# Grouped attention's projections as rounded products of 512 columns, with six heads of a row tile handled at once

## The reference

```
lat = split_cols((rms_norm_2(h, norm_g) * (1 + scale) + shift) @ w_in)      # 2048 rows
cx  = split_cols((rms_norm_2(hc, norm_g) * (1 + scale_c) + shift_c) @ w_in) # 256 context rows
# gqa_branch: 4 query heads (256 columns), 2 key heads (128), 2 value heads (128), 64 wide
ql = apply_rope(rms_norm_2(to_heads(q_l, 4), q_g), cos, sin)
kl = apply_rope(rms_norm_2(to_heads(k_l, 2), k_g), cos, sin)
vl = to_heads(v_l, 2)
kc = rms_norm_2(to_heads(k_c, 2), k_g); vc = to_heads(v_c, 2)
# apply_rope: x1, x2 = even, odd columns -> x1*cos - x2*sin, x1*sin + x2*cos
```

## Time and profile before

| | |
|---|---|
| time, median of 3 runs | 5102.38 us (5096.63 to 5104.45) |
| the profiled execution, its own time | 5105.85 us |
| span of its trace | 5104.0 us |
| PE (TensorE) busy | 4619.4 us, 91% |
| DVE busy | 2552.7 us, 50% |
| ACT busy | 1812.8 us, 36% |
| POOL busy | 1248.8 us, 24% |
| mean granted TensorE clock | 0.957 of full speed |

### The profile page before, as it was taken

How to read it: one execution, slowest core, us unless ns; L and a number is a source line. 1 busy time by engine, 2 the same in 40 slices (tenths; PEclk the granted TensorE clock), 3 DMA queues, 4 the chain that set the end, 5 groups by cost and what they waited for, 6 DMA issues and landing times. The chain is left out here.

```text
span 5104.0 us, 69099 instructions
## 1 busy us (share of the span) xinstructions
PE 4619.4 (91%) x26793; PEld 3262.8 (64%) x26793; DVE 2552.7 (50%) x5079; ACT 1812.8 (36%) x3472; POOL 1248.8 (24%) x1295
## 2 busy tenths in 40 slices
PE   6998998997969988999998998999898999989989
PEld 3447776775758656844556776877666745556767
DVE  3332245666644656445554474444655545533654
ACT  3332224663344111224444443243112224444431
POOL 1000022103410111418882000001222448850000
PEclk8999999998979999899999999999998999999999
DMA  5011103344420000100000202310000100002122
GB/s 198 8 41 71 61 1 129 135 154 163 154 95 26 1 10 1 59 15 11 11 11 29 74 29 87 91 38 17 1 10 20 48 9 11 11 14 71 44 83 91
DMA packets 150104, 272.24 MB, mean 53 GB/s; under 512 B 11756, under 2 KB 83092, under 8 KB 148116
## 3 DMA queue, kind: packets, MB, share of 16 engines
q1 hardware_dynamic: 145460, 257.34, 15.0%
q10 hardware_dynamic: 4320, 10.49, 0.6%
HBM read 198.50 MB, written 69.29 MB: 52 GB/s over the span
## 5 line engine op out<-in xcount | busy, mean ns | idle before, releaser
L1549 PE MATMUL ps_proj<-features_high,weights_high 128*128 128x512 f32 (+1 forms) x1168 | 470.9, 403 | 53.1 <-DVE features_low L1615 50.6
L1549 PE MATMUL ps_proj<-features_high,weight_ring_low 128*128 128x512 f32 (+1 forms) x1168 | 450.6, 386 | 0.0
L1549 PE MATMUL ps_proj<-features_low,weights_high 128*128 128x512 f32 (+1 forms) x1168 | 443.9, 380 | 0.0
L1615 DVE TENSOR_TENSOR features_low<-h_t,features_high 128x512 fp32r<-128x512 f32 (+2 forms) x300 | 224.3, 758 | 253.0 <-ACT features_high L1579 252.4
L1615 DVE TENSOR_TENSOR features_low<-features_or_outputs,features_high 128x512 fp32r<-128x512 f32 (+1 forms) x248 | 199.9, 816 | 228.0 <-ACT features_high L1579 227.5
L1549 PEld LDWEIGHTS ps_proj<-features_high,weights_high 128*128 128x128 f32 x1168 | 222.5, 190 | 120.9 <-issue 39.0
L1766 PE MATMUL ps_s<-qf,kb 64*128 64x128 f32 x3264 | 235.7, 285 | 60.8 <-DVE scores_t L1936 55.4
L1579 ACT ACTIVATE features_high<-h_t 128x512 fp32r<-128x512 f32 (+2 forms) x300 | 198.7, 665 | 257.8 <-PE ps_proj L1549 231.2
L2553 ACT ACTIVATE weight_ring<-ps_st 128x1024 f32<-128x1024 f32 x193 | 197.8, 1025 | 250.6 <-PE ps_st L2439 242.7
L1766 PEld LDWEIGHTS ps_s<-qf,kb 64*128 64x128 f32 x3264 | 200.8, 188 | 111.9 <-issue 59.2
L1579 ACT ACTIVATE features_high<-features_or_outputs 128x512 fp32r<-128x512 f32 (+1 forms) x248 | 176.3, 714 | 227.8 <-PE ps_proj L1549 202.4
(11 more groups left out here) (440 smaller groups left out, 10230.7 us busy)
## 6 DMA issues: line engine op xcount, KB each, us to landing
weight_ring<-in_w_in_dram SPq DMA_DIRECT2D x40, 1024.0 KB, 5.9
weight_ring<-in_w_mod_dram SPq DMA_DIRECT2D x48, 512.0 KB, 4.2
x_res<-h_rows SPq DMA_DIRECT2D x32, 512.0 KB, 4.2
res<-result SPq DMA_DIRECT2D x48, 264.0 KB, 2.1
res_rows<-res SPq DMA_DIRECT2D x48, 264.0 KB, 3.9
h_t<-v_rows SPq DMA_DIRECT2D x3, 4096.0 KB, 13.8
q_rows<-q_rows SPq DMA_DIRECT2D x34, 256.0 KB, 2.6
x_rows<-in_x_dram SPq DMA_DIRECT2D x16, 512.0 KB, 9.5
```

The costliest lines, as they stand in the source:

```text
L1549: mm = pe.matmul(bank[:, 0:n], w_[:, k0 + k, i * P:(i + 1) * P], f_[:, k, 0:n], start=start, stop=stop)
L1615: dve.tensor_tensor(self.fl[:, s % NB, :, 0:n], self.hT[:, k0:k0 + KS, c0:c0 + n], self.fh[:, s % NB, :, 0:n].bitcast(F32), ALU.subtract). ...
```

## The change

`stage_qkv2` now goes over 18 row tiles, each with all six heads and the values side by side in one PSUM bank of 512 columns. The products become split ones. A tile has two steps of four feature chunks; a step has for every chunk one product of 512 columns with `features_high`, two of 256 columns with the low weights (the ring holds the two groups apart), and one of 512 with `features_low`. `features_high` and `features_low` have two buffers, one step each, so the pair for a step can be made only when the step two before it is done. The high weights of both groups are made at the start of the stage. Queries are computed for all 18 tiles in both layers.

On ACT the new work is `rounded(s)` (high features of a step) and, once, four copies of weights; on DVE it is `low_step(s)` and, once, four subtractions:

```
+            rounded(0)
+            for half in range(2):
+                ks = slice(half * KS, (half + 1) * KS)
+                for g in range(2):
+                    w = env.group_here(act, g0 + g)
+                    act.activation(wh[:, ks, g * GC:(g + 1) * GC], w[:, ks, :], ACT.Copy).then_inc(whs.h, 1)
+            rounded(1)
...
+            def low_step(s):
+                t, k0 = s // 2, KS * (s % 2)
+                dve.wait_ge(fhs.h, fhs.at(s + 1))
+                if s >= 2:
+                    dve.wait_ge(stp.h, stp.at(s - 1))
+                dve.tensor_tensor(fl[s % 2][:, :, :], hT[:, k0:k0 + KS, t * P:(t + 1) * P], fh[:, s % 2, :, :].bitcast(F32),
+                                  ALU.subtract).then_inc(fls.h, 1)
```

POOL's addition of a tile now comes in two parts, keys first, both behind the tile's power:

```
+            def add(t):
+                pool.wait_ge(rp.h, rp.at(t + 1))
+                for g, dst, h0, nh in ((1, nat[:, t % NK, :], 4, 2), (0, qn[:, t % NQ, :], 0, 4)):
...
+                    pool.tensor_tensor(dst.rearrange("p (h x e) -> p h x e", x=2, e=HD), twice(ta), twice(tb), ALU.add).then_inc(st.h, 1)
+
+            for t in range(WT):
+                pool.wait_ge(mn.h, mn.at(t + 1))
+                pool.tensor_tensor(ss[:, 2, t, :], ss[:, 1, t, :], env.mhalf[:, :].to_broadcast([P, NH]), ALU.pow).then_inc(pw.h, 1)
+                if t >= 1:
+                    add(t - 1)
```

More of the change, by code:

```diff
@@ L2094, in stage_hgrn_norm, with stage_qkv2 @@
         s_.base += c_
-def stage_qkv2(env, layer, hT, q_d, room, spare, KA, KB, VN, qtiles):
+def stage_qkv2(env, layer, hT, q_d, room, spare, KA, KB, VN, aT, qtiles):
     nc, A = env.nc, env.A
     g0 = env.next_group
[L2105 to L2108, removed]
+    NQ, NK, KS = 3, 4, 4
+    NH, HW = 6, 6 * HD
+    NS = 2 * WT
+    fhs, fls, whs, wls, stp = (env.sem(n) for n in ("features_high", "features_low", "weights_high", "weights_low", "step_mm"))
+    nrm, rp, st = env.sem("qk_normed"), env.sem("rope_read"), env.sem("rope_sum")
     sq, mn, pw, vv = env.sem("qk_sq"), env.sem("qk_mean"), env.sem("qk_rstd"), env.sem("v_kept")
@@ L2144, in _, with turn @@
         def _(pe):
[L2145 to L2149, removed]
+            def turn(t):
+                pe.wait_ge(st.h, st.at(2 * t + 2))
                 if t >= NK:
@@ L2154, in turn @@
                 mm.then_inc(tq.h, 1)
[L2156 to L2172, removed]
@@ L2176, in _, with rounded @@
+            for t in range(WT - 2, WT):
+                turn(t)
         @block.scalar
         def _(act):
[L2178 to L2181, removed]
+            def rounded(s):
+                t, k0 = s // 2, KS * (s % 2)
+                if s >= 2:
+                    act.wait_ge(stp.h, stp.at(s - 1))
+                act.activation(fh[:, s % 2, :, :], hT[:, k0:k0 + KS, t * P:(t + 1) * P], ACT.Copy).then_inc(fhs.h, 1)
@@ L2194, in _ @@
                 act.activation(KB[HD:HD + 1, kv, :].rearrange("p (t c) -> p t c", c=P), one, ACT.Copy)
[L2195 to L2205, removed]
+            for t in range(WT):
+                if t + 1 < WT:
+                    rounded(2 * t + 2)
+                act.wait_ge(stp.h, stp.at(2 * t + 2))
+                if t >= 1:
+                    act.wait_ge(mn.h, mn.at(t))
+                act.activation(s2, ps[t % 4][:, 0:HW], ACT.Square).then_inc(sq.h, 1)
+                act.activation(VN[:, t, :], ps[t % 4][:, HW:CH], ACT.Copy).then_inc(vv.h, 1)
+                if t + 1 < WT:
+                    rounded(2 * t + 3)
+                if t >= 3:
+                    high(t - 3)
+            for t in range(WT - 3, WT):
+                high(t)
         @block.vector
@@ L2227, in low @@
                    .then_inc(kl.h, 1)
[L2229 to L2244, removed]
+            low_step(0)
@@ new lines, in _ @@
+            for half in range(2):
+                ks = slice(half * KS, (half + 1) * KS)
+                for g in range(2):
+                    dve.wait_ge(whs.h, whs.at(2 * half + g + 1))
+                    raw, lo = (r[:, (g0 + g) % 2, ks, :] for r in (env.wring, env.wlow))
+                    dve.tensor_tensor(lo, raw, wh[:, ks, g * GC:(g + 1) * GC].bitcast(F32), ALU.subtract).then_inc(wls.h, 1)
+            low_step(1)
+            dve.wait_ge(ld.h, ld.at(16 * (1 + NH)))
+            v3 = lambda a: a.rearrange("p (h e) -> p h e", e=HD)
@@ new lines, in _ @@
+            v4 = lambda a: a.rearrange("p (h j x) -> p h j x", j=32, x=2)
+            for t in range(WT):
+                if t + 1 < WT:
+                    low_step(2 * t + 2)
+                dve.wait_ge(sq.h, sq.at(t + 1))
+                link(dve.tensor_reduce(ss[:, 0, t, :], v3(s2), AXX, ALU.add))
+                dve.tensor_scalar(ss[:, 1, t, :], ss[:, 0, t, :], 1.0 / HD, EPS, ALU.mult, ALU.add).then_inc(mn.h, 1)
+                if t + 1 < WT:
+                    low_step(2 * t + 3)
+                dve.wait_ge(pw.h, pw.at(t + 1))
+                if t >= 2:
+                    dve.wait_ge(st.h, st.at(2 * (t - 1)))
+                dve.wait_ge(vv.h, vv.at(t + 1))
+                a_, b_ = ta[:, t % 2, :], tb[:, t % 2, :]
+                dve.tensor_tensor(v3(nn), v3(ps[t % 4][:, 0:HW]), ss[:, 2, t, :, None].to_broadcast([P, NH, HD]), ALU.mult)\
+                   .then_inc(nrm.h, 1)
+                dve.wait_ge(nrm.h, nrm.at(t + 1))
@@ L2256, in _ @@
                                              op0=ALU.mult, op1=ALU.mult)
[L2257 to L2261, removed]
+                    link(dve.tensor_tensor(v4(b_)[:, :, :, 1], v4(nn)[:, :, :, 0], sinv, ALU.mult))
+                dve.sem_inc(rp.h, 1)
+                if t >= 3:
+                    low(t - 3)
@@ L2262, in _ @@
+            for t in range(WT - 3, WT):
+                low(t)
             link.close()
```

111 lines of the change are left out of this document (58 added, 53 removed).

## The result

The change makes the kernel slower, inside the range that was given: 5121.72 us (median of 7 runs, 5118.47 to 5126.05) against 5104.45 for the kernel before, measured beside it (7 runs, 5096.63 to 5114.40). The ratio is 1.0035, with a 95% interval from 1.0025 to 1.0045: 17 us (13 to 23), where 25 were forecast. The profiled execution has a span of 5124.2 us, 20.2 more than before.

The account below looks back on a forecast made before the run. DVE and POOL, holding each other, were taken to pace tiles at 7.25 us. Layers' 8.0 and 15.6 plus 1.3 for a queued read made 24.9 us over 5102.4: 5127 us, range 5098 to 5142 (own range 5117 to 5137).

Parts of the forecast that it names:

- TensorE after the change: Products of one row tile on TensorE: two steps of 2.8 us, with two transposes about 5.8 us a tile.
- A tile: One row tile on DVE and POOL, which hand each other the memory: 7.25 us, against 5.8 on TensorE.
- both holdings: POOL's additions hold DVE's two-SBUF-operand instructions until they end; `low_step`, begun 0.16 us ahead, holds the power by 0.4 us.
- The sum's terms: Stage 8.0 us longer in the first layer, 15.6 in the second, 1.3 for queued reads: 24.9 us slower.
- the later read of the queries: Next stage's first read queues behind the final `q_rows` store and weight load in the first layer: 0 to 3.3, taken 1.3 us.
- The head: Stage start: first product waits 7.9 us for weights, tile 0's products end at 16.3, its sum starts at 17.0 us.
- the tail: From the last square to the stage's end: the old 7.5 us plus what six heads add, 9.65 us.
- Half the holding: Rival: the power is not held by `low_step`; tiles take 6.85 us, total 5115 us; chance 0.20.
- Late gains: Rival: gains load at 2.4 us each at the stage's start, 6 us more a layer, total 5139 us; chance 0.10.
- No holding: Rival: DVE and POOL do not hold each other; 12.5 us for two tiles, about 5097 us, no change; chance 0.14.
- TensorE the bound: Rival: POOL's additions fall where DVE reads PSUM, `low_step` always ready; tiles take 5.8 us, total 5084 us; chance 0.09.
- The change doesn't do what it says: Rival: 256-column products take 0.19 instead of 0.12 us, TensorE needs 6.9 a tile; no other time, no chance given.

Follow-up runs that it names:

- the later chain: Changed kernel with scale, gain and rope products run one tile later on DVE, transposes three tiles behind waiting for the key addition alone: 5082.86 us, ratio 0.9954.
- Short additions: Changed kernel with POOL's query addition covering only 2 of the 64 columns of each head: 5101.82 us, ratio 0.9987.
- `low_step` moved into the power: Changed kernel with a key tile's two PSUM-reading subtractions put between the mean and the second `low_step`, which so begins later: 5103.10 us, ratio 0.9994.

## Why the prediction was right, and what was off

**TensorE after the change.** Two steps and two transposes were forecast at 5.8 us, and with nothing in the way a tile takes 5.81. That forecast needed a DVE cycle of 6.2 or less, which the change's order doesn't reach; the later chain does, with the rope products free of the additions.

**A tile.** 7.25 was forecast and 7.14 measured, by the steps foreseen: power 1.71 (1.73), rope pair 1.59 (1.57), the first rope product up to 1.34 (1.3). The gain product took 0.56 in place of 0.6, since it began just as the key addition ended; its own end, 3.71 us behind the sum's start, is where the layout had it (3.77). The query addition took 1.66 where near 1.5 was foreseen, since it stood behind the gain product, and ended 4.86 us behind the sum's start (4.89). Short additions and `low_step` moved into the power show both holdings by experiment: the addition held the rope products, `low_step` the power. The prediction read the first of them from two later stages; in the second of these the DVE product of 0.88 began at 2473.82 while this pair ran, which ended at 2474.15:

```profile
2471.63 2.52 POOL L2583 TENSOR_TENSOR features_or_outputs<-features_or_outputs,probs_t 128x512 f32<-128x512 f32 x2
```

**The sum's terms.** Forecast 24.9, by stages 5.4 + 13.0 and 0.9 for the later read of the queries, 19.3 in the profile (the next stage's first product stands 2229.01 - 2225.30 = 3.71 us behind its beginning; in the trace of before it is the row below, 2220.56 - 2217.75 = 2.81). Another 0.9 of the span's 20.2 lies elsewhere and was not followed.

```profile
2220.56 1.08 PE L2396 MATMUL ps_mix<-ident,q_rows 128*128 128x128 f32 x4 [6.24 <-DMA q_rows<-q_rows]
```

The step that was mis-sized most is the tile cycle: 120.4 us from tile 0's sum to tile 17's, which were 118.7. 13 tiles take 7.14, and tile 16 takes 6.61, where all 14 were put at 7.25; the prediction overlooked that tile 16 is of context rows, which have no rope products. The head was put 1.0 us too long: first product at 7.9 (7.3; 0.4 of that is the load, 4.9 in place of 5.3), first sum at 17.0 (16.0). The last square comes at 2215.62 and the tail is 9.68 from there (9.65). Head and tiles are 2.7 us a layer, and with 0.4 of the read they make up the difference to the 24.9, but for rounding.

**The rivals.** *Half the holding* falls with the power of 1.71 beside 1.32 and 1.33 where no `low_step` begins ahead. *Late gains* falls with the `low_step` at 2094.86, released by ACT. *No holding* falls with the rope pair; what it would have given, 12.5 for two tiles, is near the 12.8 that the short addition left, with the power still held. *TensorE the bound* was the right limit for another order: its sum put it at 5084, and the later chain took 5082.86. *The change doesn't do what it says* falls with the tile of 5.81 there: the products of 256 columns cost what they cost among themselves.

## What to carry to other kernels

When products get faster, look at what the faster engine waits for, and lay out one tile on DVE and POOL with the holding between them; its durations alone said 5.9 us here and no loss. A short result that another engine makes (a power of 1.3 to 1.7 us) is hidden by working on the tile before in the meantime; here the same order also moved the additions off the rope products, and both together, with the transposes one tile later, were worth some 40 us without one instruction less. And a stage that needs all its weights at its first product wants them asked for one stage ahead.

## What was not expected of the hardware

A POOL power on 128x6 that had begun held neither of the two DVE instructions with two SBUF operands that ran wholly inside it: `low_step` (0.67, with the subtractions ahead) and the gain product (0.56, in the later chain) took their usual time. POOL's additions of 256 and 512 columns did hold `low_step` (0.77 in the later chain) and the rope products (1.59 for two, 0.63 without). The other way round a `low_step` that begins 0.10 to 0.17 us ahead of the power costs it about 0.4 us (1.71 to 1.78 in place of 1.32). And a semaphore that POOL set ahead of the power did not put the power first: DVE's instruction began 0.10 us before POOL's own next one.
